# Seven block products in place of eight in the MLP up product, and attention divisions on GpSimd, in a two-layer streaming encoder step

## The reference, cut to what matters

```
def sq_relu_mlp(h, w_up, w_down):
    return jnp.square(jax.nn.relu(h @ w_up)) @ w_down
...
    p = jax.nn.softmax(logits, axis=-1).astype(v.dtype)
    return jnp.einsum('bhqk,bkhd->bqhd', p, v)
...
    x = x + sq_relu_mlp(rmsnorm(x, norm_ffn[l]), w_up[l], w_down[l])
```

## Time and profile before

| | |
|---|---|
| median of 3 runs | 1673.44 us |
| the profiled execution: time, span | 1673.03 us, 1671.2 us |
| TensorE busy | 1584.1 us (95% of the span), 11210 matmuls |
| VectorE busy | 888.0 us (53%) |
| ScalarE busy | 629.0 us (38%) |
| GpSimd busy | 111.6 us (7%) |
| mean granted clock of TensorE | 0.974 of full speed |
| DMA | 146 MB moved, mean 87 GB/s |

### The profile page before, as it was taken

The page is one execution under the profiler, slowest core; times in us unless marked ns, Lnnn a source line. Parts: engine busy times, 40 slices in busy tenths (PEclk is TensorE's granted clock), DMA queues, the critical chain, the costliest instruction groups (busy, mean ns, idle before and its releaser), DMA issues.

```text
span 1671.2 us, 28828 instructions
## 1 busy us (share of the span) xinstructions
PE 1584.1 (95%) x11210; PEld 1496.5 (90%) x11210; DVE 888.0 (53%) x1578; ACT 629.0 (38%) x1132; POOL 111.6 (7%) x153
## 2 busy tenths in 40 slices
PE   4999979998999999999999897999899999999997
PEld 3787768887999999999999686888899999999997
DVE  4232048896345545555465246889535555555544
ACT  3313148875322222222233435887533222222213
POOL 2110011110200000000000001111020000000000
PEclk8999979999999999999999998999999999999998
DMA  7245332213212222122120536221322232231101
GB/s 258 92 133 160 122 97 58 57 29 101 76 62 90 77 74 100 53 98 75 47 70 10 190 135 205 64 63 32 102 76 76 76 100 72 78 100 58 67 0 57
DMA packets 119309, 145.99 MB, mean 87 GB/s; under 512 B 17633, under 2 KB 95521, under 8 KB 119249
## 3 DMA queue, kind: packets, MB, share of 16 engines
q1 hardware_dynamic: 119248, 145.16, 26.9%
HBM read 120.54 MB, written 24.60 MB: 87 GB/s over the span
## 4 chain that ended last, share of the span: by engine, by line
PE 58%; issue 29%; DVE 7%; ACT 4%; DMA 1%; POOL 1%; SPq 0%; DVEq 0%; POOLq 0%; ACTq 0%
PE ps L1373 50%; DVE nmx L1077 2%; DVE ptl L1102 2%; ACT pth L792 2%; PE ps L1538 2%; PE ps L1582 1%; PE ps L1584 1%; PE ps L1583 1%; PE ps L1553 1%; DVE ol L1113 1%; POOL sacc L613 1%; DVE prob L1091 1%; ACT oh L803 0%; ACT prob L782 0%; ACT wh L698 0%
## 5 line engine op out<-in xcount | busy, mean ns | idle before, releaser
L1225 DVE TENSOR_TENSOR xT<-xT,ps 128x592 f32<-128x592 f32 (+1 forms) x256 | 195.3, 763 | 189.4 <-PE ps L1373 188.1
L698 ACT ACTIVATE wh<-raw 128x2048 fp32r<-128x2048 f32 (+1 forms) x90 | 167.1, 1872 | 235.0 <-PE ps L1373 234.9
L977 DVE TENSOR_TENSOR wl<-raw,wh 128x2048 fp32r<-128x2048 f32 (+1 forms) x90 | 200.8, 2243 | 76.3 <-ACT wh L698 76.2
L1373 PE MATMUL ps<-hh,wh 128*128 128x296 f32 (+1 forms) x1024 | 221.9, 298 | 0.0
L1373 PE MATMUL ps<-xgh,wh 128*128 128x296 f32 (+1 forms) x1024 | 221.9, 298 | 0.0
L1373 PE MATMUL ps<-xgl,wh 128*128 128x296 f32 (+1 forms) x1024 | 221.2, 297 | 0.0
L1373 PE MATMUL ps<-hl,wh 128*128 128x296 f32 (+1 forms) x1024 | 220.8, 297 | 0.0
L1373 PE MATMUL ps<-xgh,wl 128*128 128x296 f32 (+1 forms) x1024 | 220.3, 296 | 0.0
L1373 PE MATMUL ps<-hh,wl 128*128 128x296 f32 (+1 forms) x1024 | 220.0, 296 | 0.0
L863 ACT ACTIVATE hh<-hw 128x592 fp32r<-128x592 f32 (+1 forms) x64 | 44.3, 693 | 351.2 <-DVE hw L1209 351.2
L1373 PEld LDWEIGHTS ps<-hl,wh 128*128 128x128 f32 x1024 | 166.1, 188 | 0.0
(11 more groups left out here) (196 smaller groups left out, 2721.0 us busy)
## 6 DMA issues: line engine op xcount, KB each, us to landing
raw<-in_w_up SPq DMA_DIRECT2D x32, 1024.0 KB, 5.5
raw<-in_w_down SPq DMA_DIRECT2D x32, 1024.0 KB, 4.9
raw<-in_w_in_a SPq DMA_DIRECT2D x12, 1024.0 KB, 7.3
kv_mla<-stn SPq DMA_DIRECT2D x24, 256.0 KB, 2.1
raw<-in_w_o_a SPq DMA_DIRECT2D x4, 1024.0 KB, 7.5
natk<-kv_mla SPq DMA_DIRECT2D x8, 512.0 KB, 4.2
raw<-in_w_o_b SPq DMA_DIRECT2D x4, 1024.0 KB, 11.0
q_mla<-stn SPq DMA_DIRECT2D x16, 192.0 KB, 1.9
```

The lines of the kernel that those rows point to most:

```text
L698: s.activation(wh[:, j % 4, 0:r * c], raw[:, j % 4, 0:r * c], ACT.Copy).then_inc(hi_done, 1)
L977: v.tensor_tensor(wl[:, j % 4, 0:r * c], raw[:, j % 4, 0:r * c], wh[:, j % 4, 0:r * c].bitcast(F32), ALU.subtract).then_inc(lo_done, 1)
L1225: v.tensor_tensor(a, a, two_banks(2 + m % 2, n), ALU.add).then_inc(x_ready if last else acc_done, 1)
L1373: return te.matmul(out, a, b, start=start, stop=stop)
```

## The change

**The up product.** A chunk's up product is seen as a 2 x 2 product of blocks: two halves of 128 hidden units, two halves of the 1024 inputs (4 k-steps each), two halves of the tokens. Before, these are eight block products. Now they are seven (`PRODUCTS`), each of 4 k-steps x 3 terms x one token half = 12 matmuls. Three are formed with sums of weight blocks (`S1` to `S4`, four sums, of which three go to `ssum` and one into `raw`), and sums of input blocks (`T1` to `T4`, made once for each layer in `operands`, from `xT`). GpSimd makes the weight sums for each chunk (`weight_sums`, four tensor_tensor of 512 elements each, L812 to L820 of the new kernel). The products are accumulated in four banks (`P_BANK`); ScalarE snapshots the first (`snap`), VectorE forms the four output blocks with five additions (`combine`, new L1476) into `hu`, in which norm and squares then work.

**Weights of the MLP** are converted in pieces of 512 elements: seven of up (`up_hi`, `up_lo`) and four of down (`down_hi`, `down_lo`) for a chunk, in place of two pieces of 2048. Each has a slot of its own in `wuh`/`wul`, `dn1h`, `dn2h`. `raw` holds two chunks of up weights, one of down weights, and `ssum`. The output projection now uses two of the four slots of `wh`/`wl` (`w_slot`), since the others hold `T` operands.

**TensorE's order** in the MLP is the same, up of c+1, down of c, and so on; up now waits for `snap_done` and `u_add` in mid product, since banks 0, 1 and 2 are used on. The norm factors (`spread_rstd`) are spread after the whole first up product and no longer inside it.

**Attention.** `scale` on VectorE and `scale3` on ScalarE are gone. GpSimd does all five multiplications of a head (`normalise`, new L744), as a tensor_tensor of `prob` with `rs` broadcast along the row. The splitting of V is cut in three parts that lie between them.

The core of the diff:

```diff
@@ gpsimd
+            def normalise(layer, h, c, u):
+                n = unit_keys(u)[1]
...
+                pool.wait_ge(recip_done, h * 5 + (5 * HEADS * layer + u + 1))
+                g.tensor_tensor(prob[0:rows, c, off:off + n], prob[0:rows, c, off:off + n],
+                                rs[0:rows, u:u + 1].to_broadcast([rows, n]), ALU.mult).then_inc(p_ready, 1)
...
+            def weight_sums(layer, c, par, first=False):
...
+                    pool.wait_ge(ul_done, c * 7 + (7 * c0 - 2))
+                g.tensor_tensor(ssum[:, 1, :, :], a11, a21, ALU.subtract).then_inc(s_ready, 1)
+                g.tensor_tensor(a21, a21, a22, ALU.add).then_inc(s_ready, 1)
+                g.tensor_tensor(ssum[:, 0, :, :], a21, a11, ALU.subtract).then_inc(s_ready, 1)
...
+                g.tensor_tensor(ssum[:, 2, :, :], ssum[:, 0, :, :], a12, ALU.subtract).then_inc(s_ready, 1)
@@ scalar, period(c)
-                def scale3(h, c):
...
+                    act.wait_ge(p_ps, c * 7 + (7 * c0 + 7 + 1))
+                    s.activation(snap[:, 0, 0:h], ps[:, 0, 0:h], ACT.Copy).then_inc(snap_done, 1)
@@ vector, operands(layer): for each block m of the output projection
+                    v.tensor_tensor(a, a, two_banks(m % 2, n), ALU.add).then_inc(x_ready, 1)
+                    if m < 4:
+                        scaled(t1f[:, k, 0:h], m, first, b12[:, k, 0:h], ALU.subtract)
+                        lo_x("B11", k, m, first)
+                        lo_tmp("T1", k, t1f[:, k, 0:h])
+                    else:
+                        scaled(t24[:, 0:h], m, second, t1f[:, k, 0:h], ALU.add)
+                        scaled(t3f[:, 0:h], m, second, b12[:, k, 0:h], ALU.subtract)
+                        lo_x("B21", k, m, first)
+                        lo_x("B22", k, m, second)
+                        lo_tmp("T2", k, t24[:, 0:h])
+                        scaled(t24[:, 0:h], m, first, t24[:, 0:h], ALU.subtract)
+                        lo_tmp("T3", k, t3f[:, 0:h])
+                        lo_tmp("T4", k, t24[:, 0:h])
+                    if m in (2, 4):
+                        lo(j0 + 1 + m // 2)
@@ vector, attention
-                def scale(h, c, u):
...
-                    scale(h, c, 1)
@@ tensor, mlp(layer)
+                    for u in range(7):
+                        bank, what = P_BANK[u], P_OPERAND[u]
+                        pe.wait_ge(ul_done, c * 7 + (7 * c0 + u + 1))
...
+                        if u == 3:
+                            pe.wait_ge(snap_done, c + (c0 + 1))
+                        if u == 4:
+                            pe.wait_ge(u_add, c * 5 + (5 * c0 + 1))
+                        if u == 6:
+                            pe.wait_ge(u_add, c * 5 + (5 * c0 + 3))
...
+                            for p, (w, x) in enumerate(((w_h, x_h), (w_h, x_l), (w_l, x_h))):
+                                i = te.matmul(ps[:, bank, 0:h], w[:, k, :], x, start=(u not in (3, 4, 6) and k == 0 and p == 0),
...
+                    if first:
+                        spread_rstd(layer)
```

More of the change, by code:

```diff
@@ L671, in _, with attention, head, head_and_v @@
-            sum_squares(1)
-            rstd(1)
+                if part == 2:
+                    i.then_inc(v_split, 1)
+            def attention(layer):
+                def head(h, c):
+                    for u in range(5):
+                        normalise(layer, h, c, u)
+                def head_and_v(h, c, j, slot, turn):
+                    for u in range(3):
+                        normalise(layer, h, c, u)
+                        split_v(layer, j, slot, turn, u, True)
+                    normalise(layer, h, c, 3)
+                    normalise(layer, h, c, 4)
+                for j in range(2):
+                    for part in range(3):
+                        split_v(layer, j, j, 0, part)
+                for h in range(4):
+                    head(h, h % 2)
+                with pool.Fori(0, PAIRS // 2 - 1) as i:
+                    head_and_v(4 * i + 4, 0, 2 * i + 2, 0, i + 1)
+                    head(4 * i + 5, 1)
+                    head_and_v(4 * i + 6, 0, 2 * i + 3, 1, i + 1)
+                    head(4 * i + 7, 1)
@@ new lines, in mlp_sums @@
+            def mlp_sums(layer):
+                b = 2 * layer + 1
+                for k in range(1, 5):
+                    add_squares(b, k)
+                weight_sums(layer, 0, 0, True)
+                for k in range(5, KD):
+                    add_squares(b, k)
+                weight_sums(layer, 1, 1, True)
+                rstd(b)
+                with pool.Fori(0, NCH // 2 - 1) as i:
+                    weight_sums(layer, 2 * i + 2, 0)
+                    weight_sums(layer, 2 * i + 3, 1)
@@ L724, in gain_hi @@
                                  scale=gT[:, gain + k:gain + k + 1]).then_inc(y_scaled, 1)
-            def square_and_gain(b, gain, pieces=None):
-                for k in range(KD):
-                    gain_hi(b, k, gain)
-                    square(b, k)
-                    if pieces is not None and k in (2, 4, 6):
-                        hi(pieces + k // 2 - 1)
             act.wait_ge(gT_ready, 1)
@@ L817, in step @@
                             turned(h, u)
-                        if u == 0 and not first:
-                            scale3(h - 1, 1 - c)
                         if u == 2 and not (isinstance(h, int) and h < 2):
@@ L886, in _ @@
+            operands(0, 8)
+            mlp(0)
+            for j in range(KVD0, QD0 + 1):
+                hi(j)
             for k in range(KD):
@@ L940, in _ @@
             attention(1)
-            for q in range(4):
-                hi(WO_B0 + q)
-            square_and_gain(3, 32, MLP_B0)
-            mlp(1, MLP_B0, False)
+            operands(1, 32)
+            mlp(1)
             for k in range(KD):
@@ L1272, in _ @@
             attention(0)
-            for q in range(4):
-                lo(WO_A0 + q)
-            residual_and_gain(1, WO_A0, 8, T)
-            mlp(0, MLP_A0, None, True)
+            operands(0, 8)
+            mlp(0, None)
             lo(QD0)
@@ L1356, in _ @@
             attention(1)
[L1357 to L1360 removed]
+            operands(1, 32)
+            mlp(1, 40)
             variance(4, 6)
```

644 lines of the change are left out of this document (418 added, 226 removed).

## The result

Medians: 1677.28 us before (6 runs), 1664.12 us after (6 runs), ratio 0.992 with a 95% interval of 0.9895 to 0.9947. The change is faster by 13 us, where 41 were forecast, and the time lies above the range.

What follows compares the result with a forecast made beforehand. TensorE's matmul issue was taken to bound the MLPs, a ring of three nearly full engines the attention. 1673.0 - 51.6 + 3 + 22 + 2 - 16 = 1632 us, range 1610 to 1656.

Steps and rivals of the forecast that it cites:

- Fewer matmuls: Both MLPs: 192 fewer matmuls in each, at unchanged cost per matmul, save 51.6 us.
- Case E: Rival, up product: 84 matmuls take the time of 96, so 1684 us; chance 0.03.
- Steady loop: MLP loops: VectorE keeps up beside GpSimd's sums; 3 us lost over both loops, with ends 0 and 15.
- Case D: Rival, MLP loops: GpSimd's sums delay the first combine, fifth product 2.3 us late a chunk, 1701 us; chance 0.05.
- The way into the MLP: Output projection and first two up products: VectorE runs late, costing 11 us a layer, 22 in both; ends 5 and 17.
- TensorE's pauses do not lower its clock: Way into the MLP: idle TensorE keeps its clock, as in 376 to 400 us, 7.6 of 24 us idle at 0.99.
- Way out of MLP 0: End of MLP 0: two latent pieces of 1.5 us each stand ahead of the last adds, costing 2 us.
- Attention, -16: Attention: relief of VectorE and ScalarE gives back 0.5 us a head over 32 heads, 16 us (0 to 35).
- Case A: Rival, attention: gives nothing, the ring being set by TensorE and ScalarE's exponential, so 1648 us; chance 0.12.
- C: Rival, MLPs: way in costs its upper end and loops lose 0.5 us a chunk, so 1656 us; chance 0.08.

Runs made afterwards that it cites:

- e3: Changed kernel with GpSimd's weight sums and sums of squares in the MLP cut to one column (values not the reference's): 1643.5 us, ratio 0.9795 to before.
- e12: Changed kernel with seven weight-sum operations a chunk on GpSimd in place of four, the extra three read by nothing: one execution of 1710.6 us.
- e9: Changed kernel with the MLP entry reordered, chunk 0's last combination ahead of spreading and normalisation, and both ends edited; nothing left out: 1632.7 us, ratio 0.975 to before.
- e13: e9's kernel with GpSimd's work in the MLP cut to one column (sums and statistics not formed): 1622.0 us, ratio 0.967 to before.
- e5: Changed kernel with the third latent piece's high part behind ScalarE's gains and pair 1's V split behind head 0's divisions: 1660.2 us, ratio 0.992 to before.
- e1: Kernel before with only the attention edit (divisions on GpSimd, V split in three), no seven-product scheme: 1670.2 us, ratio 0.997 to before.
- e8: Changed kernel with each attention division on GpSimd cut to one column (values not the reference's), all waits kept: one execution of 1665.8 us.
- e6: Changed kernel with the MLP entry reordered, chunk 1's weight sums ahead of the inverse root, plus both edits of e5: 1649.6 us, ratio 0.985 to before.
- e2: Changed kernel with the attention of the kernel before, so only the seven-product up product: 1668.1 us, ratio 0.995 to before.
- e11: Changed kernel with only the way out of MLP 0 edited, first two latent pieces split in the period before the last: 1660.3 us, ratio 0.9915 to before.

## Why the prediction was wrong

The direction and two of the five terms were right; the sum missed by 32 us in the median and 22 in the profiled execution. In the profile the two entries are 17.5 us over their forecast and the two stretches with attention 6.7, and the rests of the MLPs 2.4 under.

- **Fewer matmuls, -51.6: right.** 84 up matmuls a chunk at 0.1364 and 0.1326 us, twelve in one bank at no loss. Case E is out.
- **Steady loop, +3: right, it was 0**, though contention is there (VectorE is busy 20.07 us a chunk where I counted 17; in e3 73.9 of 100 us for 81.7, which is 1.9 us a chunk, and a split takes 0.68 us where I put 0.60). Case D did not happen, and e12 shows that it was near.
- **"The way into the MLP", +22: the step that failed.** The entries lost 98.7 - 75.3 = 23.4 us and 96.8 - 72.9 = 23.9 against their matmuls, where the kernel before lost 81.9 - 78.6 = 3.3 and 80.5 - 76.1 = 4.4: +39.6. I counted each delay by itself and took contention for the middle of its bounds; I named 17 a layer as the end "if each of eight GpSimd instructions also stops VectorE for 1.28". There are twelve sums and seven square sums in the stretch, VectorE is the engine that all wait for there, and a late split meets the next GpSimd sum. e3 puts 19.8 of it on GpSimd's work beside VectorE's, of which it doesn't separate the port from the length of the sums. e9 puts 21.6 on the order, with GpSimd's work as it was (33 us in each entry); the two overlap (together, e13, 32.5). With the order right the entry costs 88.1 + 85.8 against 148.2 of matmuls, 18 us over the kernel before: about what I had forecast for the order that was given.
- **"TensorE's pauses do not lower its clock": wrong.** One row of pauses does not make a rule, and the row that I took ends where the clock fell. The kernel before, right behind it, after a wait of 5.2 us:

```profile
400.00:403.00 3.00, 3.00 (x13) 3.00 (x14) 3.00 (x2) 2.70 (x2) 0.00 (x0) 0.50 0.67 186
```

Behind the projection of entry 0 the clock was down for 3.4 and 6.8 us, in which TensorE was busy 3.4 and 3.9: some 3.7 us of loss, and 1.7 in entry 1. In e3 and e9 it stayed at 1.00 there, so a part of what they gained is clock.
- **Way out of MLP 0, +2: it was +3.4**, and I had the cause right in the prediction (two pieces ahead of the last adds), then looked elsewhere for it in e5.
- **Attention, -16: mis-sized.** It gave 5.5 us by itself (e1, by the interval 3.4 to 7.5), and 7.3 by the outputs of the heads: 0.30 us a steady head where I took 0.5. TensorE's wait of 2.3 us for the first division is not shown to cost anything: in e5 it is gone, and the ratio is that of the change. Case A, where "the ring is set by TensorE and by ScalarE's exponential", was nearer. I read the waits of the weight loads as what can come back; 0.84 us of their 1.1 a head are still there: of the four only the first shrank, by 0.27 us, about what the head gained. e8 shows that the length of the divisions is not what holds it. What of TensorE's busy 87.8 of 88 us is work and what is modelled end of a matmul the trace does not tell, so which of TensorE's issue and the exchange of copies sets the 9.80 us stays open.
- **Rivals and range.** The time that came is that of no case: entries beyond the end of C, attention between the forecast and A, the loops at no loss. C and A together, 1656 + 16, would have held it; I let the range end at C alone, as if the cases excluded each other. The terms were independent, and two of them at their bad ends are not rare.

## What to carry to other kernels

Work that is given to GpSimd is paid by VectorE too where VectorE reads two SBUF operands, here with 1.0 to 1.1 us for an instruction of 1.4 to 1.6; in a loop with slack ahead of the critical instruction that cost nothing, in a start-up where VectorE is the engine that all wait for 19.8 us of 34.6 came through. Order VectorE's queue at such a place by who waits: first what frees a bank of TensorE's, then splits, then what only VectorE needs; here that was worth 22 us in the two entries, of 31 in the median, without an instruction less. Idle time per iteration is not slack: what counts is the part ahead of the one instruction that TensorE waits for.

## What the runs showed of the hardware

- A VectorE instruction with two SBUF inputs waits out most of one of GpSimd's: 0.52 us became 1.55, the 512-element split 0.68 became 1.78, and GpSimd's own sum went from 1.27 to 1.62. One with an input in PSUM keeps its time: `xT` 0.77 us at 440.56 and `snap` 0.45 at 465.98, both beside a sum. The Trainium skill says so (SBUF — State Buffer, "Who interferes with whom"); this kernel's traces agree, and show that both sides are lengthened.
- The granted clock fell to 0.50 in the changed kernel's wait of 5.0 us and was back 3.9 us after it ended. In e9, with 19.8 of 24 us busy from 450 us on and waits of up to 2.4 us, it did not fall in the entry; nor in e3. When it falls stays open.
- At one place the same wait of 3.6 us was followed by a clock of 1.00 in some executions and of 0.84 in others over the next 18 us (e5 and the changed kernel; e3 and e6): 2 us that no instruction explains. The same holds for longer stretches: e8, with the changed kernel's instructions in its input and latent products, had a clock of 0.95 for 0.97 up to 220 us and 0.91 for 0.95 from 870 to 1005 us, and came 4.0 us later to the output projection and 3.4 us later through the latent stage and attention 1. Single stretches of two profiles are no surer than that; entry 0, 98.7 to 100.0 us in the five profiles with its order unchanged (the changed kernel, e2, e5, e8, e11), varies far less than what e3 and e9 took off it.
- A multiplication on GpSimd with one operand spread from a column costs less than the subtraction that I priced it by: 1.07 us for 528 elements where 1.32 was worked out, 3.7 us for a head's five in place of 4.5.
